# One-hot masks for four tokens in one VectorE operation, the gate weights put on by ScalarE

## The chip, the cores and the metric

One core of one Trainium2 chip. The metric is the device time of one execution, in microseconds (us), the median of the runs. The engines are called PE (TensorE), DVE (VectorE), ACT (ScalarE), POOL (GpSimd) and SP (SyncE, here only a DMA queue).

## What is computed

Two transformer blocks on 256 tokens of width 1024, in float32: a mixer with sparse attention and a state space model, feed-forward layers, a short convolution, a second mixer, and at the end `peer_ffn`, a feed-forward layer over 16384 experts of which each token and head picks 16. The change lies in that last layer:

```python
idx = jnp.take_along_axis(cand_i, pos, axis=-1)      # expert = i1 * 128 + i2
gate = jax.nn.softmax(top_s, axis=-1)
...
hid = jnp.einsum('thkd,td->thk', u[ib], xb)
a = jax.nn.gelu(hid.astype(jnp.float32), approximate=False) * gb
return jnp.einsum('thk,thkd->td', a.astype(x.dtype), v[ib])
```

## The kernel before, in words

The expert layer is computed densely for 224 of the 256 tokens (T): all 16384 experts, 128 at a time, with a matrix of gates that is zero where a token did not pick an expert. The gate matrix of one token is 128 x 128 (first key by second key), and is the product of two matrices with one row for each of its 128 picks: the first row is a one-hot of the first key times the gate, the second a one-hot of the second key. The other 32 tokens are done by fetching the rows of their picks ("picks" below).

The stage that the change touches (`peer_build` in the stream's phases) runs over 56 groups of four tokens. Groups are numbered 0 to 55. In a group:

- DVE, `one_hots(n)`: waits until the scatter of group n - 2 is done (the two buffers alternate), and writes the first one-hots of four tokens into `OH1` (L2780, one operation for a token: compare with `iota`, a row 0 to 127 that lies in PSUM, then multiply by the gate) and the second ones into `OH2` (L2783, one operation for the four). Both are parts of `XN`; `OH1` is `XN[:, 0]`, `OH2` is `XN[:, 1]`. `selT` holds, for each token as a column, the first key, the second key and the gate.
- PE, `scatter`: waits for the one-hots, and multiplies them, four matmuls into one PSUM bank (L1395).
- ACT: copies the first 48 columns of each token's gates out of the bank (L1975).
- DVE, `weigh(n)`: waits for that copy, and multiplies the other 80 into the activations that lie there (L2793).

Six groups of seven also carry one unit of weights (48 units in all, a unit is 128 experts by 1024): a group whose number is divisible by 7 carries none. For each unit a DMA brings 128x1024 floats into a ring of four, ACT rounds each half to the high part (L1475, `round_unit`, called through `follow`, which works two units ahead), POOL subtracts to get the low part (L665), and PE multiplies (L789, L790). ACT then copies the low product out of the bank (L1989, event `build_low`), DVE adds it to the high one (L2805, `summed_build`, event `build_sum`), and ACT takes the gelu of the unit before (L1967, `staged`), which is spilled to memory.

On 20 of the groups DVE also does one pick (L2763): a multiply with a sum over 128x1024, both operands in SBUF. POOL starts the fetch of its rows (L677).

Everything is ordered by hand: each engine runs its own list, and waits on semaphores. DVE's list in this stage is, for n from 2 on, `one_hots(n)`, `weigh(n - 2)`, `summed_build(n - 2)`, and the pick if there is one. `one_hots(0)` and `one_hots(1)` come eight units earlier. ACT's list for group n is the copy L1975, the two roundings of the unit two ahead, the copy L1989, and the gelu L1967. After the stage come 128 units of the last product (L1419, L1421), and the end.

Of the kernel before, what the change touches and what calls it, by code (L numbers as in the profile page):

```python
# [20 lines left out]
ALU = mybir.AluOpType  # L21
ACT = mybir.ActivationFunctionType
# [5 lines left out]
P = 128  # L28
# [39 lines left out]
GROUPS_OF_4 = T // 4  # L68
# [179 lines left out]
def build(nc, stream, x, vec, row, row2, kv_w, br_w, key_w, u_rows, v_rows, gain_row, spill, out):  # L248
    ctx = ExitStack()

    def sb(name, shape, dt=F32):
        return ctx.enter_context(nc.sbuf_tensor(name, shape, dt))

    def sem(name):
        return ctx.enter_context(nc.semaphore(name))

    with ctx:
# [3 lines left out]
        XN = sb("XN", [P, NT, D])  # L261
# [18 lines left out]
        selT = sb("selT", [P, 3, S])  # L280
# [125 lines left out]
        OH1 = XN[:, 0, :].rearrange("p (b n k) -> p b n k", b=2, n=4)  # L406
        OH2 = XN[:, 1, :].rearrange("p (b n k) -> p b n k", b=2, n=4)
# [21 lines left out]
        def ev(name):  # L429
            if name not in events:  # L430
                events[name] = sem(name)
            return events[name]
# [28 lines left out]
        def unit_used(phase, e, i=0):  # L461

            return halves_used, number(phase, e, i, 2, 2)
# [4 lines left out]
        def before_turn(name, i=0):  # L468

            bank, n, _ = TURNS[name]  # L470
            return bank_free[bank], i + n

        def fills(name):
            return bank_full[TURNS[name][0]], 1

        def full(name, i=0):
            bank, _, n = TURNS[name]
            return bank_full[bank], i + (n + 1)
# [4 lines left out]
        def read_out(name, i=0):  # L483

            bank, n, _ = TURNS[name]
            return bank_free[bank], i + (n + 1)

        def bank(name):
            return psum[TURNS[name][0]]
# [238 lines left out]
        def _(pe):  # L728
# [623 lines left out]
            def experts():  # L1352
# [35 lines left out]
                def scatter(g, i):  # L1388

                    j = i * BUILD_GROUPS + g  # L1390
                    name = f"G{j % 4}"
                    pe.wait_ge(*before_turn(name, j // 4))
                    pe.wait_ge(ev("one_hot"), j + 1)
                    for n in range(4):
                        last = mm(bank(name)[:, n * P:(n + 1) * P], OH1[:, j % 2, n, :], OH2[:, j % 2, n, :],  # L1395
                                  start=True, stop=True)
                    last.then_inc(*fills(name))

                for i in range(BUILD_ITERS):
                    for g in range(BUILD_GROUPS):  # L1400
                        scatter(g, i)
                        if g % PERIOD:
                            e = (PERIOD - 1) * (g // PERIOD) + g % PERIOD - 1
# [29 lines left out]
                for half in range(2):  # L1433
                    cols = slice(half * HALF, (half + 1) * HALF)
                    first, second = f"picked_rows{half}", f"picked_rows{2 + half}"
# [3 lines left out]
                    for c in range(4):  # L1439
                        k, at = 4 * half + c, slice(c * P, (c + 1) * P)  # L1440
# [23 lines left out]
        def _(act):  # L1464
            A = nc.scalar.activation
            chain = Chain(act, scalar_chain)

            def round_unit(phase, e, i=0, halves=range(2)):

                act.wait_ge(*unit_in(phase, e, i))  # L1470
                for k in halves:
                    if not isinstance(i, int) or 2 * (PHASES[phase].first + e) + k >= HSLOTS:

                        act.wait_ge(halves_used, number(phase, e, i, 2, k + 1 - HSLOTS))
                    A(w_hi[:, half_slot(phase, e, k), :], ring[:, slot(phase, e), k * HALF:(k + 1) * HALF],  # L1475
                      ACT.Copy).then_inc(rounded, 1)

            def follow(phase, e, i=0, halves=range(2)):

                at = PHASES[phase].first + e + AHEAD + (i * PHASES[phase].units if isinstance(i, int) else 0)  # L1480
                if at < NUNITS:
                    round_unit(phase, e + AHEAD, i, halves)
# [411 lines left out]
            def experts():  # L1894
# [45 lines left out]
                for u in range(EARLY):  # L1940
# [10 lines left out]
                    for t, after in enumerate((32, 58)):  # L1951
                        if u == after:
                            act.wait_ge(ev("top_diff"), t + 1)
                            A(TS[:, t, :, :], TS[:, t, :, :], ACT.Exp,
                              scale=stat[:, 6 + t:7 + t]).then_inc(ev("top_exp"), 1)
# [8 lines left out]
                def staged(c):  # L1964

                    act.wait_ge(ev("build_sum"), c + 1)
                    A(stage[:, c % STAGED, :], bank(f"build{c % 3}")[:, 0:T],  # L1967
                      ACT.Gelu).then_inc(*frees(f"build{c % 3}"))

                act.wait_ge(ev("pick_index_in"), 16 * LANES)  # L1970
                act.wait_ge(ev("pick_gate_in"), 16 * LANES)
                for n in range(GROUPS_OF_4):
                    i, g = n // BUILD_GROUPS, n % BUILD_GROUPS
                    act.wait_ge(*full(f"G{n % 4}", n // 4))
                    A(G[:, 0:GATED, 4 * n:4 * n + 4],  # L1975
                      bank(f"G{n % 4}")[:].rearrange("p (t k) -> p k t", t=4)[:, 0:GATED, :],
                      ACT.Copy).then_inc(ev("gates_copied"), 1)
                    if g % PERIOD:
                        e = (PERIOD - 1) * (g // PERIOD) + g % PERIOD - 1
                        c = i * BUILD_UNITS + e  # L1980
                        follow("peer_build", e, i)
                        if c == GATED - 1:
                            for q in range(4):
                                act.wait_ge(*read_out(f"G{q}", GROUPS_OF_4 // 4 - 1))
                            A(A_hi[:, 0, 0:T], G[:, GATED, :], ACT.Copy).then_inc(ev("late_high"), 1)
                        if c >= STAGED:
                            act.wait_ge(ev(f"spilled{c % STAGED}"), 16 * (c // STAGED))
                        act.wait_ge(*unit_used("peer_build", e, i))
                        A(stage[:, c % STAGED, :], bank(f"build{c % 3}")[:, T:2 * T], ACT.Copy).then_inc(ev("build_low"), 1)  # L1989
                        if c:  # L1990
                            staged(c - 1)
                staged(GATED - 1)
# [49 lines left out]
            mixer2()  # L2042
            norm_late(6, "norm2")
            experts()


        @block.vector
        def _(dve):
            V = nc.vector
# [610 lines left out]
            def experts():  # L2660
# [13 lines left out]
                for t in range(NT):  # L2674
# [40 lines left out]
                    places = psum[3][:, 0:256].rearrange("p (k f) -> p k f", k=2)  # L2715
# [29 lines left out]
                iota = bank("iota")[:, 0:P]  # L2745
# [28 lines left out]
                def one_hots(n):  # L2774

                    if n >= 2:
                        dve.wait_ge(*full(f"G{(n - 2) % 4}", (n - 2) // 4))
                    for k in range(4):
                        tok = 4 * n + k
                        V.tensor_scalar(OH1[:, n % 2, k, :], iota, selT[:, 0, tok:tok + 1],  # L2780
                                        selT[:, 2, tok:tok + 1], ALU.is_equal, ALU.mult)
                    second = selT[:, 1, 4 * n:4 * n + 4]
                    V.tensor_tensor(OH2[:, n % 2, :, :], iota.unsqueeze(1).broadcast_to([P, 4, P]),  # L2783
                                    second.unsqueeze(2).broadcast_to([P, 4, P]),
                                    ALU.is_equal).then_inc(ev("one_hot"), 1)

                def weigh(n):
# [18 lines left out]

                one_hots(0)
                one_hots(1)
                summed_early(8)
                for n in range(2, GROUPS_OF_4):  # L2810
# [186 lines left out]
```

## Time and profile before

| | us |
|---|---|
| median of 3 runs (lowest, highest) | 1683.74 (1679.53, 1688.74) |
| the profiled execution | 1680.42 |
| its span | 1678.7 |
| PE busy | 1630.7 (97%) |
| DVE busy | 1050.8 (63%) |
| ACT busy | 973.3 (58%) |
| POOL busy | 1129.6 (67%) |

The profile counts an engine as busy from the start of an instruction to its end, the last part of which can lie over the next instruction. So a row "x4" of four like instructions is shorter than four times one. Times in the rows are from the start of the span. An idle time in brackets is that just before the instruction, with the instruction that ended it.

### The profile page before, as it was taken

The numbers are of one execution on the slowest core, as the hardware profiler recorded it, in microseconds if no ns is written. First come the engines' busy times: TensorE is split into PE (matmuls) and PEld (weight loads), VectorE is DVE, ScalarE is ACT, GpSimd is POOL, SyncE is SP. The second block draws the span as 40 slices with busy tenths as digits, with TensorE's granted clock in tenths as the row PEclk, the third lists the DMA queues.
The fourth block names the chain that finished last, engine by engine and source line by source line (L and its number), as shares of the span: only waits on it lengthen the run. The fifth ranks groups of instructions, "written<-read, shape, count | busy, mean of one in ns | idle before, by whom it ended". The sixth has DMA issues, their size and how long they took to land.

```text
span 1678.7 us, 30573 instructions
## 1 busy us (share of the span) xinstructions
PE 1630.7 (97%) x10334; PEld 1489.0 (89%) x10334; DVE 1050.8 (63%) x2318; ACT 973.3 (58%) x1962; POOL 1129.6 (67%) x897
## 2 busy tenths in 40 slices
PE   8999999999999999999999999998999999999998
PEld 8888888889988888899998989998899899998997
DVE  2784433334243333754523589995999888787997
ACT  5556655555465555666545667665555566665664
POOL 8445799998989999886536799998888711111110
PEclk9999999999999999999999999999999999999999
DMA  6333455554545555443333465655677788788994
GB/s 231 102 107 108 156 188 189 188 187 169 187 165 190 187 187 190 168 155 138 127 151 118 161 215 194 205 200 203 209 249 236 234 276 301 268 278 285 325 333 162
DMA packets 102012, 332.52 MB, mean 198 GB/s; under 512 B 11888, under 2 KB 24304, under 8 KB 101648
## 3 DMA queue, kind: packets, MB, share of 16 engines
q1 hardware_dynamic: 91152, 292.07, 50.5%
q0 software_dynamic: 9696, 37.91, 7.4%
q10 hardware_dynamic: 1056, 1.16, 0.3%
q8 instruction: 60, 0.98, 0.2%
q14 instruction: 48, 0.39, 0.1%
HBM read 323.98 MB, written 6.55 MB: 197 GB/s over the span
## 4 chain that ended last, share of the span: by engine, by line
PE 72%; POOL 9%; DVE 9%; issue 6%; ACT 2%; DMA 1%; POOLq 0%; SPq 0%; DVEq 0%; ACTq 0%
PE bank L757 27%; PE bank L789 12%; PE bank L1419 12%; POOL w_lo L665 9%; PE bank L790 6%; PE bank L1421 6%; DVE XN L2780 3%; DVE arena L2763 1%; PE bank L735 1%; DVE XN L2783 1%; DMA ring<-stream 1%; PE bank L1395 1%; PE bank L1307 1%; DVE arena L2793 1%; ACT w_hi L1475 1%
## 5 line engine op out<-in xcount | busy, mean ns | idle before, releaser
L665 POOL TENSOR_TENSOR w_lo<-ring,w_hi 128x512 fp32r<-128x512 f32 x804 | 1045.7, 1318 | 249.5 <-ACT w_hi L1475 214.1
L1475 ACT ACTIVATE w_hi<-ring 128x512 fp32r<-128x512 f32 x1060 | 662.8, 630 | 524.9 <-PE bank L790 239.9
L789 PE MATMUL bank<-h_high_and_low,w_hi 128*128 128x448 f32 (+1 forms) x1728 | 584.2, 389 | 8.8 <-POOL w_lo L665 8.8
L790 PE MATMUL bank<-h_high_and_low,w_lo 128*128 128x224 f32 (+1 forms) x1728 | 468.4, 271 | 0.0
L789 PEld LDWEIGHTS bank<-h_high_and_low,w_hi 128*128 128x128 f32 x1728 | 326.0, 189 | 59.7 <-POOL w_lo L665 12.4
L790 PEld LDWEIGHTS bank<-h_high_and_low,w_lo 128*128 128x128 f32 x1728 | 329.7, 191 | 1.6
L1419 PE MATMUL bank<-A_high_and_low,w_hi 128*128 128x448 f32 x1024 | 322.9, 376 | 4.4 <-DVE A_high_and_low L2835 4.3
L757 PE MATMUL bank<-h_high_and_low,w_hi 128*128 128x256 f32 x1504 | 286.3, 288 | 4.2 <-POOL w_lo L665 3.5
L1421 PE MATMUL bank<-A_high_and_low,w_lo 128*128 128x224 f32 x1024 | 270.0, 264 | 0.0
L757 PEld LDWEIGHTS bank<-h_high_and_low,w_hi 128*128 128x128 f32 x1504 | 241.2, 194 | 7.7 <-issue 3.8
L757 PE MATMUL bank<-h_high_and_low,w_lo 128*128 128x256 f32 x752 | 214.8, 286 | 0.0
L1419 PEld LDWEIGHTS bank<-A_high_and_low,w_hi 128*128 128x128 f32 x1024 | 192.7, 188 | 20.2 <-DVE A_high_and_low L2835 5.2
L1421 PEld LDWEIGHTS bank<-A_high_and_low,w_lo 128*128 128x128 f32 x1024 | 195.9, 191 | 0.0
L2828 DVE TENSOR_TENSOR w_lo<-ring,w_hi 128x512 fp32r<-128x512 f32 x256 | 175.9, 689 | 30.2 <-ACT w_hi L1475 19.7
L677 POOL DMA_INDIRECT arena<-v_rows,rows x32 | 37.5, 1172 | 191.4 <-DVE arena L2770 158.2
L757 PEld LDWEIGHTS bank<-h_high_and_low,w_lo 128*128 128x128 f32 x752 | 146.3, 195 | 1.0 <-issue 0.7
L757 PE MATMUL bank<-w_hi,A_high_and_low 128*128 128x512 f32 x432 | 143.0, 392 | 0.6 <-DVE A_high_and_low L2460 0.3
L2452 DVE TENSOR_TENSOR bank<-bank,arena 128x256 f32<-128x256 f32 x44 | 19.0, 433 | 146.5 <-ACT arena L1751 146.3
L757 PE MATMUL bank<-w_hi,h_high_and_low 128*128 128x512 f32 (+1 forms) x336 | 102.5, 379 | 2.3 <-POOL w_lo L665 2.0
L757 PEld LDWEIGHTS bank<-w_hi,A_high_and_low 128*128 128x128 f32 x432 | 81.1, 188 | 19.7 <-DVE A_high_and_low L2460 1.2
L2009 ACT ACTIVATE A_high_and_low<-arena 128x224 fp32r<-128x224 f32 x127 | 49.6, 391 | 63.8 <-PE bank L1421 60.7
L757 PE MATMUL bank<-w_lo,A_high_and_low 128*128 128x512 f32 x216 | 84.6, 392 | 0.0
(387 smaller groups left out, 1906.6 us busy)
## 6 DMA issues: line engine op xcount, KB each, us to landing
ring<-stream SPq DMA_DIRECT2D x530, 512.0 KB
spill<-mask_parts SPq DMA_DIRECT2D x48, 112.0 KB
XN<-spill SPq DMA_DIRECT2D x48, 112.0 KB, 5.7
arena<-branch_w POOLq DMA_DIRECT2D x1, 3072.0 KB, 12.9
X<-x SPq DMA_DIRECT2D x2, 512.0 KB, 4.8
arena<-kv_w SPq DMA_DIRECT2D x1, 1024.0 KB, 6.7
out<-X SPq DMA_DIRECT2D x4, 256.0 KB, 2.2
arena<-row POOLq DMA_DIRECT2D x1, 512.0 KB, 4.5
```

The source lines that it names most:

```text
L665: nc.gpsimd.tensor_tensor(w_lo[:, hs, :], ring[:, slot(phase, e), k * HALF:(k + 1) * HALF], w_hi[:, hs, :].bitcast(F32), ALU.subtract) \
L677: nc.gpsimd.indirect_dma_start(fetched[:, s % FETCH, :], None, (u_rows if s < PICKED else v_rows), bass.IndirectOffsetOnAxis(pick_index[:, ...
L757: last = mm(dst, a, b, start=start and n == 0, stop=stop and n == 2, skip_group_check=True)
L789: mm(dst[:, 0:2 * n], high, h[:, k, :, 0:n], start=k == 0, stop=False, skip_group_check=True)
L790: last = mm(dst[:, 0:n], low, h_hi[:, k, 0:n], start=False, stop=k == KC - 1, skip_group_check=True)
L1419: mm(dst[:, 0:2 * T], high, A2[:, :, n % 2, 0:T], start=n == 0, stop=False, skip_group_check=True)
L1421: last = mm(dst[:, 0:T], low, A_hi[:, n % 2, 0:T], start=False, stop=n == NKEYS - 1, skip_group_check=True)
L1475: A(w_hi[:, half_slot(phase, e, k), :], ring[:, slot(phase, e), k * HALF:(k + 1) * HALF], ACT.Copy).then_inc(rounded, 1)
L2009: A(A_hi[:, nxt % 2, 0:T], chunk(GATED + nxt if nxt < EARLY else nxt - EARLY), ACT.Copy).then_inc(ev("late_high"), 1)
L2452: chain(V.tensor_tensor(gate[:, 0:S], gate[:, 0:S], LOW[:, q % 2, 0, :], ALU.add))
L2780: V.tensor_scalar(OH1[:, n % 2, k, :], iota, selT[:, 0, tok:tok + 1], selT[:, 2, tok:tok + 1], ALU.is_equal, ALU.mult)
L2828: V.tensor_tensor(w_lo[:, hs, :], ring[:, slot(phase, e), k * HALF:(k + 1) * HALF], w_hi[:, hs, :].bitcast(F32), ALU.subtract) \
```

## The change

DVE compares `iota` with the first and the second keys of four tokens in one operation over 128x1024 elements, which gives both masks as zeros and ones. ACT multiplies the first mask by the gates in place, one operation for a token (`weighted`), and counts `first_weighted`. PE's scatter waits for that instead of `one_hot`. ACT does groups 0 and 1 ahead of its loop, and group n + 2 right after the copy of group n. The rounding of a unit's second half moves behind the copy L1989 (L2002 in the changed kernel).

```diff
@@ scatter
-                    pe.wait_ge(ev("one_hot"), j + 1)
+                    pe.wait_ge(ev("first_weighted"), j + 1)
@@ ACT
+                def weighted(n):
+
+                    if n < GROUPS_OF_4:
+                        act.wait_ge(ev("one_hot"), n + 1)
+                        for k in range(4):
+                            tok = 4 * n + k
+                            ins = A(OH1[:, n % 2, k, :], OH1[:, n % 2, k, :], ACT.Copy,
+                                    scale=selT[:, 2, tok:tok + 1])
+                        ins.then_inc(ev("first_weighted"), 1)
+
+                weighted(0)
+                weighted(1)
                 for n in range(GROUPS_OF_4):
...
                       ACT.Copy).then_inc(ev("gates_copied"), 1)
+                    weighted(n + 2)
                     if g % PERIOD:
...
-                        follow("peer_build", e, i)
+                        follow("peer_build", e, i, (0,))
...
                         A(stage[:, c % STAGED, :], bank(f"build{c % 3}")[:, T:2 * T], ACT.Copy).then_inc(ev("build_low"), 1)
+                        follow("peer_build", e, i, (1,))
                         if c:
                             staged(c - 1)
@@ DVE, one_hots
-                    for k in range(4):
-                        tok = 4 * n + k
-                        V.tensor_scalar(OH1[:, n % 2, k, :], iota, selT[:, 0, tok:tok + 1],
-                                        selT[:, 2, tok:tok + 1], ALU.is_equal, ALU.mult)
-                    second = selT[:, 1, 4 * n:4 * n + 4]
-                    V.tensor_tensor(OH2[:, n % 2, :, :], iota.unsqueeze(1).broadcast_to([P, 4, P]),
-                                    second.unsqueeze(2).broadcast_to([P, 4, P]),
+                    both = XN[:, :, n % 2 * 4 * P:(n % 2 + 1) * 4 * P].rearrange("p w (n k) -> p w n k", n=4)
+                    places = selT[:, 0:2, 4 * n:4 * n + 4]
+                    V.tensor_tensor(both, iota.unsqueeze(1).unsqueeze(1).broadcast_to([P, 2, 4, P]),
+                                    places.unsqueeze(3).broadcast_to([P, 2, 4, P]),
                                     ALU.is_equal).then_inc(ev("one_hot"), 1)
```

ACT's list at the begin of the stage, before. The first row is the last of the stage ahead; L1975 is the copy of a group's gates (groups 0 and 1, then 2), L1475 the two roundings, L1989 the copy of the low product, L1967 the gelu:

```order
L1919 ACTIVATE arena<-bank 128x224 x2
L1975 ACTIVATE arena<-bank 128x48x4 x2
L1475 ACTIVATE w_hi<-ring 128x512 x2
L1989 ACTIVATE mask_parts<-bank 128x224
L1975 ACTIVATE arena<-bank 128x48x4
L1475 ACTIVATE w_hi<-ring 128x512 x2
L1989 ACTIVATE mask_parts<-bank 128x224
L1967 ACTIVATE mask_parts<-bank 128x224
```

The same place now; L1978 puts the gates on (groups 0 and 1 at the head, then 2, 3, 4), L1987 is the copy of the gates, L2002 the copy of the low product:

```order
L1919 ACTIVATE arena<-bank 128x224 x2
L1978 ACTIVATE XN<-XN,selT 128x128 x8
L1987 ACTIVATE arena<-bank 128x48x4
L1978 ACTIVATE XN<-XN,selT 128x128 x4
L1987 ACTIVATE arena<-bank 128x48x4
L1978 ACTIVATE XN<-XN,selT 128x128 x4
L1475 ACTIVATE w_hi<-ring 128x512
L2002 ACTIVATE mask_parts<-bank 128x224
L1475 ACTIVATE w_hi<-ring 128x512
L1987 ACTIVATE arena<-bank 128x48x4
L1978 ACTIVATE XN<-XN,selT 128x128 x4
L1475 ACTIVATE w_hi<-ring 128x512
```

Four operations of ACT now stand between the copy of a group's gates and the copy of a unit's low product, and the second rounding stands behind that.

DVE's list from group 1's sum on, before (then all of one pass, with its pick, and the next masks; L2780 and L2783 the one-hots, L2793 `weigh`, L2805 `summed_build`, L2763 the pick):

```order
L2805 TENSOR_TENSOR bank<-bank,mask_parts 128x224
L2780 TENSOR_SCALAR XN<-bank,selT 128x128 x4
L2783 TENSOR_TENSOR XN<-bank,selT 128x512
L2793 TENSOR_TENSOR arena<-arena,bank 128x80x4
L2805 TENSOR_TENSOR bank<-bank,mask_parts 128x224
L2763 SCALAR_TENSOR_TENSOR arena,rows<-arena 128x1024
L2780 TENSOR_SCALAR XN<-bank,selT 128x128 x4
L2783 TENSOR_TENSOR XN<-bank,selT 128x512
```

And now (L2794 both masks, L2804 `weigh`, L2816 `summed_build`, L2777 the pick):

```order
L2816 TENSOR_TENSOR bank<-bank,mask_parts 128x224
L2794 TENSOR_TENSOR XN<-bank,selT 128x2x512
L2804 TENSOR_TENSOR arena<-arena,bank 128x80x4
L2816 TENSOR_TENSOR bank<-bank,mask_parts 128x224
L2777 SCALAR_TENSOR_TENSOR arena,rows<-arena 128x1024
L2794 TENSOR_TENSOR XN<-bank,selT 128x2x512
```

Five operations have become one, and the order of the rest stands: the sum of a unit, and the pick, still come ahead of the next group's masks.

## Rows read from the trace of the kernel before

**Rows 1.** Busy time by stretch: stretch, length, busy PE, PEld, DVE, ACT, POOL, clock, DMA
```profile
1180.00:1200.00 20.00, 19.08 (x138) 18.31 (x137) 20.00 (x52) 11.15 (x30) 17.72 (x14) 1.00 0.65 214
...
1380.00:1500.00 120.00, 119.86 (x765) 114.07 (x764) 98.76 (x168) 73.33 (x145) 19.46 (x17) 1.00 0.82 281
```

**Rows 2.** Groups by shape, 1160 to 1338 us: busy us, mean ns, idle before
```profile
L1395 PE MATMUL bank<-XN 128*128 128x128 f32 x444 | 59.3, 277 | 8.3 <-DVE XN L2783 8.2
L2763 DVE SCALAR_TENSOR_TENSOR arena<-arena 128x1024 f32<-128x1024 f32 x20 | 36.8, 1839 | 0.0
```

**Rows 3.** Timeline of DVE, one group with a unit: start us, length us
```profile
1221.09 1.36 DVE L2780 TENSOR_SCALAR XN<-bank,selT 128x128 f32<-128x128 f32 x4
1222.38 0.68 DVE L2783 TENSOR_TENSOR XN<-bank,selT 128x512 f32<-128x512 f32 x1
1222.97 0.47 DVE L2793 TENSOR_TENSOR arena<-arena,bank 128x320 f32<-128x320 f32 x1
1223.37 0.39 DVE L2805 TENSOR_TENSOR bank<-bank,mask_parts 128x224 f32<-128x224 f32 x1
1223.67 1.35 DVE L2780 TENSOR_SCALAR XN<-bank,selT 128x128 f32<-128x128 f32 x4
```

**Rows 4.** The chain of waits in order of time: start us, length us
```profile
1233.78 0.90 PE bank L1395 x8
1237.18 0.90 PE bank L1395 x8
```

**Rows 5.** Timeline of ACT: the first gate copies, and part of a group
```profile
1161.21 0.55 ACT L1975 ACTIVATE arena<-bank 128x192 f32<-128x192 f32 x2
...
1202.06 0.63 ACT L1475 ACTIVATE w_hi<-ring 128x512 fp32r<-128x512 f32 x1 [0.56 <-PE bank L790]
1202.60 0.34 ACT L1989 ACTIVATE mask_parts<-bank 128x224 f32<-128x224 f32 x1
1202.83 0.35 ACT L1967 ACTIVATE mask_parts<-bank 128x224 f32<-128x224 f32 x1
```

**Rows 6.** Timeline of ACT, much earlier: two 128x128 operations with a scale per partition
```profile
917.54 0.68 ACT L1492 ACTIVATE XN<-ident,stat 128x128 f32<-128x128 f32 x2
918.13 1.92 ACT L1475 ACTIVATE w_hi<-ring 128x512 fp32r<-128x512 f32 x3
```

**Rows 7.** Timelines of ACT and DVE: hand-overs between the two
```profile
1167.78 0.34 ACT L1989 ACTIVATE mask_parts<-bank 128x224 f32<-128x224 f32 x1
1168.22 0.40 DVE L2805 TENSOR_TENSOR bank<-bank,mask_parts 128x224 f32<-128x224 f32 x1 [0.19 <-ACT mask_parts L1989]
1176.10 0.39 DVE L2805 TENSOR_TENSOR bank<-bank,mask_parts 128x224 f32<-128x224 f32 x1
1176.52 0.36 ACT L1967 ACTIVATE mask_parts<-bank 128x224 f32<-128x224 f32 x1 [1.61 <-DVE bank L2805]
```

**Rows 8.** Timeline of ACT: the low copy of the stage's last unit
```profile
1341.15 0.34 ACT L1989 ACTIVATE mask_parts<-bank 128x224 f32<-128x224 f32 x1
```

**Rows 9.** Timelines of POOL and DVE around the first pick and the eighth
```profile
1165.30 7.52 POOL L665 TENSOR_TENSOR w_lo<-ring,w_hi 128x512 fp32r<-128x512 f32 x6
1168.53 5.38 DVE L2763 SCALAR_TENSOR_TENSOR arena<-arena 128x1024 f32<-128x1024 f32 x1
1225.74 1.28 POOL L665 TENSOR_TENSOR w_lo<-ring,w_hi 128x512 fp32r<-128x512 f32 x1
1226.24 1.87 DVE L2763 SCALAR_TENSOR_TENSOR arena<-arena 128x1024 f32<-128x1024 f32 x1
```

**Rows 10.** Timeline of PE at two stalls, and stretches around the first (columns as rows 1)
```profile
1147.62 0.47 PE L789 MATMUL bank<-h_high_and_low,w_hi 128*128 128x448 f32 x1 [2.41 <-POOL w_lo L665]
1141.00:1160.00 19.00, 15.91 (x92) 14.62 (x91) 6.61 (x18) 9.77 (x23) 16.10 (x13) 0.91 0.49 167
1149.00:1150.00 1.00, 1.00 (x6) 0.91 (x5) 0.02 (x1) 0.11 (x1) 1.00 (x2) 0.50 0.30 45
1175.93 1.13 PE L1395 MATMUL bank<-XN 128*128 128x128 f32 x8 [1.93 <-DVE XN L2783]
```

## The prediction, made before the changed kernel ran

> **What bounds the kernel now.** First the busy time by stretch, to see which engine fills the stage. From 1180 to 1200 us, inside the stage, DVE is busy 20.00 of 20.00 us and PE 19.08, at full clock [rows 1]. After the stage PE is busy 119.86 of 120 us [rows 1]: whatever the stage gains or loses stays in the total, since PE has nothing to catch up with. Then the groups: PE's scatter waited 8.2 us for one-hots [rows 2]. The timeline gives what each step costs in DVE's row of work, start to start: first one-hots 1.29, second 0.59, `weigh` 0.40, sum 0.30; together 2.58 us for a group with a unit, 2.28 without [rows 3]. The 20 picks add 36.8 us [rows 2]: 48 x 2.58 + 8 x 2.28 + 36.8 = 179 us, which is the stage. PE by itself needs 3.40 us for a group with a unit, since two scatters start 1233.78 and 1237.18, 0.90 of it the scatter [rows 4]: 48 x 3.40 + 8 x 0.90 = 170.4 us. So DVE bounds the stage, about 10 us above PE.
>
> **What the change takes away and adds.** DVE: five operations of 1.29 + 0.59 = 1.88 us become one of 128x1024. That shape is not there with one operand in PSUM. The 128x512 one takes 0.68 and the 128x320 one 0.47 [rows 3], so 512 elements more are 0.54, and one takes 1.21 us (start to start 1.12). Bounds: a 128x1024 row with both operands in SBUF has a mean of 1.84 [rows 2], two of 128x512 are 1.35. I take 1.21, for the new operation has the operands of L2783. DVE's row falls by 0.76 us a group, 43 us in all, far below PE. Alone that would be a gain.
>
> ACT: four operations of 128x128 with a scale per partition. Two such started 0.59 us before what followed them [rows 6]: 0.295 each, start to start, and 0.68 for both means 0.39 for the last. From below, a 128x224 copy without such a scale takes 0.23 start to start [rows 5]; from above, four of 0.39 with no overlap. I take 0.295, the same form of instruction. So four cost 1.18 us.
>
> **Who waits for that.** ACT's row stays under PE's: 0.2 for the gates, 1.18, two roundings of 0.54, copy and gelu 0.24 each [rows 5], 2.9 us. But the order of waits closes a loop through DVE and ACT in every group with a unit. ACT can't copy the low product of group m before it has put the gates on group m + 2; for that it needs DVE's masks m + 2; these stand in DVE's list behind the sum of group m - 1 and its pick; and that sum waits for the low copy of group m - 1. One turn of the loop per group, with nothing to run ahead. Its length:
> - low copy 0.34 [rows 7];
> - hand-over to DVE 0.10 (1167.78 + 0.34 to 1168.22) [rows 7];
> - sum 0.30, start to start [rows 3];
> - both masks 1.21;
> - hand-over to ACT 0.04 (1176.10 + 0.39 to 1176.52), with the other direction's 0.10 as its upper bound [rows 7];
> - four with the gates 1.18;
> - first rounding 0.54, to the next low copy [rows 5].
>
> Together 3.71 us, against PE's 3.40. Before, there was no such loop: ACT's low copy did not wait for one-hots. A pick now lies on the loop with its full length, where it was only one more piece of DVE's row. By itself a pick takes about as long as now: it starts 0.74 us after the low copy (0.34 + 0.10 + 0.30); POOL is then in the half whose rounding ended 0.09 after that copy's start, until about 1.47 (1.28 us [rows 9]); and a pick ends 1.09 after such a POOL operation (1225.74 + 1.28 to 1226.24 + 1.87) [rows 9], at 2.56. That is 1.82, start to start 1.75. A group without a unit adds masks and `weigh`, 1.12 + 0.40 = 1.52.
>
> **The sum.** The gates of group 0 can only go on once ACT has finished the stage ahead, at 1161.21, where the first gate copy now starts [rows 5]; before, PE scattered by itself. From there: 1.27 (3 x 0.295 + 0.39) and 0.1, scatter 0.90, then 0.1; masks of group 2 and `weigh` 1.52; masks of group 3 1.21; gates 1.18; rounding 0.54: the first low copy starts 6.9 later, at 1168.1. Then 45 turns of 3.71 = 167.0; the last two low copies have no gates ahead of them and go by PE, 2 x 3.40 = 6.8; 20 picks x 1.75 = 35.0; 7 groups without a unit x 1.52 = 10.6. The last low copy starts at 1387.5. Now it starts at 1341.15 [rows 8]. So +46 us on the profiled execution: 1680.4 + 46.4 = **1727 us**, 2.7% slower. The median of the runs shown is 3.3 us above the profiled execution; the sum is made against the latter.
>
> Moved at no cost: the second rounding goes 0.24 us back, behind the low copy, and waits for the same thing, the end of the group's unit. POOL has it 0.9 us after the low copy's start, and PE has to begin on that half by about 6 us after it (7.4 - 1.25, below); without that cover the loop would wait for PE. SP's loads follow POOL's splits, which only get further apart.
>
> **The clock.** PE's granted clock fell to 0.50 of full, the 1.2 GHz level, after a stall of 2.41 us, and did not fall at the stall of 1.93 that ends at 1175.93 [rows 10]. In the changed kernel PE waits about 0.3 us a group, and where a pick and a group without a unit come together 2 to 4 us, perhaps ten times, so it will fall there. One fall costs PE some 1.7 us of work (19 us at a mean of 0.91) [rows 10]. I price that at nothing: PE is off the loop, with about 3 us to spare. (Two halves split by POOL at 1.28, the second then multiplied in 1.25, end some 4.1 us after the low copy of group m; the low copy of group m + 2 wants them at 7.4.) The Trainium skill speaks of more (TensorE: Matmul & The Clock Gate, "A second HAM failure mode: psum-queue depth-cycling"): PE that idles briefly between groups of matmuls makes the clock swing between its levels, and throughput drops. By that rule PE itself could get slower than the loop; that is the third rival, and of it the one fall in [rows 10] is all that the trace shows.
>
> **The picks and POOL.** The first pick ran into a block of six POOL operations on end and took 5.38 us, to 1.1 after the block's end at 1172.82; the eighth waited for one operation only [rows 9]. In the changed kernel the second rounding is ready 0.5 us before POOL's first half ends, so POOL again has work on end. If DVE loses that hand-over each time, a pick takes 1.2 us more. The Trainium skill (SBUF — State Buffer, "Who interferes with whom") has DVE and GpSimd take a shared pair of ports for one whole instruction, the other blocked till its end; by that alone a pick waits for one POOL operation, 1.75 us as above, and the sum stands. The first pick disagrees with it, the eighth agrees.
>
> **The rivals.**
> - The gates cost ACT less. If the four go at the pace of plain copies, 0.23 as the 128x224 one or 0.14 by number of elements, the loop is 3.45 to 3.1 us and the total 1715 down to 1699. For it: plain copies of ACT do go at that pace [rows 5]. Against: the same form as the new one does not [rows 6]. Chance 0.12 for below 1715.
> - The loop doesn't hold, and PE bounds the stage: 170.4 + 3 us later start against 181 now (1161 to 1341.15 is 180), some 8 us less, **1672 us**. For it: DVE's row falls to 2.58 - 0.76 = 1.82 a group and ACT's stays under 3.40. The point from which it decides: from the first low copy at 1168.1 to the present last one there are 173.0 us, so a turn must be under (173.0 - 6.8 - 35.0 - 10.6) / 45 = 2.7 us. It would have to be a whole microsecond shorter, nearly all that the four gate operations cost; or ACT would have to have the masks a group ahead, which the order of DVE's list forbids. Chance 0.05. About the same as before, within 0.5%: 0.04.
> - PE's clock swings and PE becomes the bound. Ten to fifteen falls that no longer hide cost 1.7 each, 17 to 25 us more: 1744 to 1752. Against it: PE's 3 us to spare. Chance 0.07.
> - DVE loses the hand-over to POOL at the picks: 20 x 1.2 = 24 us, 1751. Chance 0.06.
>
> **How the numbers follow.** The forecast's own case has 0.66. Its bounds: hand-over to ACT up by 0.06 is +3; masks of 1.35 instead of 1.21 +6, of 1.84 +28; a mean pick of 1.2 or 2.1 instead of 1.75 -11 or +7; gates with no overlap +17. The range of 1703 to 1750 takes these in but for the dearest masks, which have two SBUF operands, half of the first rival and most of the third, and leaves out the fast case, no change, and the far ends, under 0.2. A measurement of this kernel tells about 0.5% (8 us) from no change, as the runs shown lie within 0.3% of their median: faster 0.05, same 0.04, slower 0.91.
>
> **What would show it.** In the changed profile: the low copies (L2002) 3.7 us apart in groups with a unit and no pick, 5.4 with one, and the last at about 1387; the masks (L2794) at 1.21 us; L1978 at 0.39 with four in 1.27; each L1978 released by DVE's L2794, each DVE sum by ACT; DVE busy some 60% of the stage (56 x 1.52 + 48 x 0.30 + 35 = 134 of 226 us) and PE near 75% (170 of 226); the chain of waits going back and forth between ACT and DVE. Wrong would be: PE without stalls at the scatter, 3.40 us between scatters, or L1978 starting without an idle time ahead of it.

## The result, and the profile after

The changed kernel takes 1720.61 us (median of 4 runs, 1720.04 to 1722.21), against 1682.21 us for the kernel before in the same series (1679.53 to 1688.74). The ratio is 1.0224, 95% interval 1.0194 to 1.0253: slower by 38.4 us. The profiled execution took 1722.21 us (span 1720.4), that of before 1680.42, so between the two traces that are compared here there are 41.8 us; the forecast was +46.4, and 1727. Among the runs of the versions below there is one of 1974.29 us, at a granted clock of 0.752, which stands in no median and no ratio here.

The page after, its busy time, the chain that ended last (shares of the span by line), and the group of the new operation (busy us, mean ns, idle before it):

```profile
PE 1649.1 (96%) x10334; PEld 1500.2 (87%) x10334; DVE 1011.0 (59%) x2094; ACT 1032.2 (60%) x2186; POOL 1137.9 (66%) x897
...
PE bank L757 26%; PE bank L1419 12%; PE bank L789 12%; POOL w_lo L665 9%; PE bank L790 6%; PE bank L1421 6%; DVE XN L2794 3%; ACT XN L1978 2%; ACT w_hi L1475 2%; PE bank L735 1%; PE bank L1395 1%; DVE bank L2816 1%; PE bank L1307 1%; DVE arena L2777 1%; PE bank L836 1%
...
L1978 ACT ACTIVATE XN<-XN,selT 128x128 f32<-128x128 f32 x224 | 71.6, 391 | 65.6 <-DVE XN L2794 65.5
```

DVE's masks, ACT's gates and ACT's first rounding now stand one behind the other on the chain. In order of time (start us, length us):

```profile
1175.51 0.40 DVE bank L2816
1175.91 1.14 DVE XN L2794
...
1177.38 0.97 ACT XN L1978 x3
1178.35 0.52 ACT w_hi L1475
1178.88 0.25 ACT mask_parts L2002
```

Busy time by stretch (columns as [rows 1]), inside the stage and behind it:

```profile
1160.00:1380.00 220.00, 191.06 (x1203) 178.48 (x1203) 135.17 (x197) 153.26 (x461) 154.02 (x118) 0.92 0.57 187
1380.00:1500.00 120.00, 119.30 (x760) 113.28 (x759) 98.53 (x175) 73.51 (x146) 18.61 (x19) 1.00 0.84 282
```

Against [rows 1]: DVE, which was busy without a gap, is now busy 61% of the stage, no engine is full in it, and the stage is 41 us longer. Behind it PE is as full as before, so the loss stays in the total. The last low copy starts at 1382.02, against 1341.15 [rows 8]: 40.9 of the 41.8 us lie ahead of it.

The groups of the stage by shape, 1160 to 1380 us (busy us, mean ns, idle before), which answer to [rows 2]:

```profile
L1978 ACT ACTIVATE XN<-XN,selT 128x128 f32<-128x128 f32 x218 | 69.8, 391 | 65.6 <-DVE XN L2794 65.5
L1395 PE MATMUL bank<-XN 128*128 128x128 f32 x446 | 66.2, 297 | 22.4 <-ACT XN L1978 22.4
L2794 DVE TENSOR_TENSOR XN<-bank,selT 128x1024 f32<-128x1024 f32 x54 | 65.6, 1215 | 3.6 <-PE bank L1395 3.6
L2777 DVE SCALAR_TENSOR_TENSOR arena<-arena 128x1024 f32<-128x1024 f32 x20 | 34.7, 1737 | 0.0
L2816 DVE TENSOR_TENSOR bank<-bank,mask_parts 128x224 f32<-128x224 f32 x47 | 18.8, 400 | 82.1 <-ACT mask_parts L2002 78.6 <-PE bank L790 3.6
```

Two waits that face each other are how a loop looks in such a table: DVE's sum waits 78.6 us for ACT's low copy, ACT's gates wait 65.5 us for DVE's masks. One turn of it in the timelines, ACT first, then DVE (start us, length us, idle before):

```profile
1175.07 0.34 ACT L2002 ACTIVATE mask_parts<-bank 128x224 f32<-128x224 f32 x1
1175.31 0.62 ACT L1475 ACTIVATE w_hi<-ring 128x512 fp32r<-128x512 f32 x1
1175.83 0.34 ACT L1967 ACTIVATE mask_parts<-bank 128x224 f32<-128x224 f32 x1
1176.07 0.32 ACT L1987 ACTIVATE arena<-bank 128x192 f32<-128x192 f32 x1
1177.07 1.28 ACT L1978 ACTIVATE XN<-XN,selT 128x128 f32<-128x128 f32 x4 [0.68 <-DVE XN L2794]
1178.26 0.62 ACT L1475 ACTIVATE w_hi<-ring 128x512 fp32r<-128x512 f32 x1
1178.78 0.34 ACT L2002 ACTIVATE mask_parts<-bank 128x224 f32<-128x224 f32 x1
```

```profile
1170.07 0.40 DVE L2816 TENSOR_TENSOR bank<-bank,mask_parts 128x224 f32<-128x224 f32 x1 [1.78 <-ACT mask_parts L2002]
1170.38 1.81 DVE L2777 SCALAR_TENSOR_TENSOR arena<-arena 128x1024 f32<-128x1024 f32 x1
1172.12 0.08 DVE L2777 DVE_READ_ACCUMULATOR arena<-arena 128x1 f32 x1
1172.12 1.21 DVE L2794 TENSOR_TENSOR XN<-bank,selT 128x1024 f32<-128x1024 f32 x1
1173.26 0.47 DVE L2804 TENSOR_TENSOR arena<-arena,bank 128x320 f32<-128x320 f32 x1
1175.51 0.40 DVE L2816 TENSOR_TENSOR bank<-bank,mask_parts 128x224 f32<-128x224 f32 x1 [1.79 <-ACT mask_parts L2002]
1175.82 1.22 DVE L2794 TENSOR_TENSOR XN<-bank,selT 128x1024 f32<-128x1024 f32 x1
```

Low copy 1175.07, sum 1175.51, masks 1175.82, gates 1177.07, rounding 1178.26, next low copy 1178.78: 3.71 us. The turn before it has the pick of 1170.38 in it and takes 5.43. Over the stage, 24 turns take 3.70, 14 with a pick 5.42 to 5.44, and 7 across a group without a unit 5.2 to 7.0.

### The profile page after: what moved, and what is told of

It is laid out like the page before. It is cut to its first block, busy times and chain, and to the rows that moved or that the text cites. A ratio compares the mean times of both kernels' runs of the same rounds, so it can differ in the third digit from the quotient of the medians.

```text
span 1720.4 us, 30621 instructions
## 1 busy us (share of the span) xinstructions
PE 1649.1 (96%) x10334; PEld 1500.2 (87%) x10334; DVE 1011.0 (59%) x2094; ACT 1032.2 (60%) x2186; POOL 1137.9 (66%) x897
## 4 chain that ended last, share of the span: by engine, by line
PE 70%; POOL 9%; DVE 7%; issue 6%; ACT 6%; DMA 1%; POOLq 0%; DVEq 0%; ACTq 0%; SPq 0%
PE bank L757 26%; PE bank L1419 12%; PE bank L789 12%; POOL w_lo L665 9%; PE bank L790 6%; PE bank L1421 6%; DVE XN L2794 3%; ACT XN L1978 2%; ACT w_hi L1475 2%; PE bank L735 1%; PE bank L1395 1%; DVE bank L2816 1%; PE bank L1307 1%; DVE arena L2777 1%; PE bank L836 1%
## 5 line engine op out<-in xcount | busy, mean ns | idle before, releaser
L1475 ACT ACTIVATE w_hi<-ring 128x512 fp32r<-128x512 f32 x1060 | 661.4, 629 | 456.8 <-PE bank L757 218.6
L789 PE MATMUL bank<-h_high_and_low,w_hi 128*128 128x448 f32 (+1 forms) x1728 | 592.9, 393 | 14.8 <-POOL w_lo L665 14.4
L677 POOL DMA_INDIRECT arena<-v_rows,rows x32 | 42.9, 1341 | 186.3 <-DVE arena L2784 153.5
L1978 ACT ACTIVATE XN<-XN,selT 128x128 f32<-128x128 f32 x224 | 71.6, 391 | 65.6 <-DVE XN L2794 65.5
L1395 PE MATMUL bank<-XN 128*128 128x128 f32 x448 | 66.5, 297 | 25.5 <-ACT XN L1978 25.5
```

Source lines behind the costliest of these rows:

```text
L677: nc.gpsimd.indirect_dma_start(fetched[:, s % FETCH, :], None, (u_rows if s < PICKED else v_rows), bass.IndirectOffsetOnAxis(pick_index[:, ...
L789: mm(dst[:, 0:2 * n], high, h[:, k, :, 0:n], start=k == 0, stop=False, skip_group_check=True)
L1978: ins = A(OH1[:, n % 2, k, :], OH1[:, n % 2, k, :], ACT.Copy, scale=selT[:, 2, tok:tok + 1])
```

## The experiments

Each is an edit of the changed kernel and runs against the kernel before; "turn" is the distance from one low copy to the next. The ratio and its 95% interval are against the kernel before in the same series, whose median was 1682.12 to 1685.01 us. That the time went into the loop is the theory. The rivals are PE's clock, the amount of ACT's added work by itself, and the picks.

**Gates late.** `weighted(n + 2)` goes to the end of ACT's pass, behind the low copy and the second rounding. The work is the same; the loop is opened.

```
-                    weighted(n + 2)
                     if g % PERIOD:
...
                             staged(c - 1)
+                    weighted(n + 2)
```

> The gates of group m + 2 go on at the end of ACT's pass for group m instead of ahead of the first rounding and the low copy; nothing is left out. Loop theory: the low copy of group m no longer waits for DVE's masks m + 2, one turn of the loop now spans two groups (3.7 us plus a gate copy, against 6.8 of PE), so PE bounds the stage: 48 x 3.40 + 8 x 0.90 = 170.4 us from the first scatter, about 51 us less than in the changed kernel, 1670 to 1676 us, and so 6 to 12 us below the kernel before. Rival A (ACT has simply too much to do, the four operations delay the roundings): the same work in another order gives the same time, 1720. Rival B (PE's clock falls are the loss): about 17 us of the 41 come back, near 1704, unless the stalls go too.

1688.28 us (1684.71 to 1692.7), ratio 1.0029 (1.0009 to 1.0049). Of the 40 turns that don't cross a group without a unit 36 are 3.40 us, with or without a pick (the other four 3.23 to 3.93), and the low copies now wait for PE:

```profile
1164.90 0.36 ACT L2001 ACTIVATE mask_parts<-bank 128x224 f32<-128x224 f32 x1 [0.40 <-PE bank L790]
1168.30 0.36 ACT L2001 ACTIVATE mask_parts<-bank 128x224 f32<-128x224 f32 x1 [0.56 <-PE bank L790]
```

So 32 of the 38 us come back by order alone, at the same 224 gate operations. It fell short of the expectation by 12 us or more, at one place: across a group without a unit the turn is 6.15 to 6.7 instead of 4.30, 14 us in all. PE gets through the empty group in 0.9 us and then waits for gates that ACT has only reached after the unit ahead (PE's timeline, the three scatters around such a group):

```profile
1201.45 1.06 PE L1395 MATMUL bank<-XN 128*128 128x128 f32 x8
1204.85 1.06 PE L1395 MATMUL bank<-XN 128*128 128x128 f32 x8
1207.54 1.13 PE L1395 MATMUL bank<-XN 128*128 128x128 f32 x8 [1.62 <-ACT XN L1978]
```

**Pick ahead.** DVE's pick goes ahead of its sum, the gates stay early.

```
                     weigh(n - 2)
-                    summed_build(n - 2)
                     if n in PICK_GROUPS:
                         pick(PICK_GROUPS.index(n))
+                    summed_build(n - 2)
```

> In DVE's list the pick stands ahead of the sum instead of behind it, where DVE now waits 1.78 us for the low copy; nothing is left out. Loop theory: 16 of the 20 picks fall into that wait and leave the loop, 16 x 1.73 = 28 us less, 1693 us; the four in groups without a unit stay. Sums of a group with a pick start 3.7 us after the last, no longer 5.4. Rival A (ACT's load): no change, 1720. Rival B (clock): the longest stalls of PE come with the picks, so most of the falls go, and with them up to 17 us, 1704.

1694.46 us (1690.41 to 1698.75), ratio 1.0061 (1.0036 to 1.0086). Nearly all turns with a pick fell from 5.43 to 3.70, the others stayed. DVE's row of work shows why: the pick now fills the time in which DVE waits for the low copy anyway, and only 0.35 us of that wait is left:

```profile
1233.19 1.51 DVE L2777 SCALAR_TENSOR_TENSOR arena<-arena 128x1024 f32<-128x1024 f32 x1
1234.62 0.08 DVE L2777 DVE_READ_ACCUMULATOR arena<-arena 128x1 f32 x1
1235.06 0.40 DVE L2816 TENSOR_TENSOR bank<-bank,mask_parts 128x224 f32<-128x224 f32 x1 [0.35 <-ACT mask_parts L2002]
```

The same 20 operations are worth 26 us by standing one instruction further on or back; from the first low copy to the last it is 188.3 us instead of 216.1.

**Two gates.** Only two of the four gate operations are left in each group; the gates of the other two tokens are left out.

```
-                        for k in range(4):
+                        for k in range(2):
```

> ACT puts the gates on the first two tokens of a group only; the other two keep plain masks, so their gates are left out. All else as in the changed kernel. Loop theory: a turn is two operations of 0.295 shorter, 3.11 us, and 4.84 with a pick; 45 turns and the first groups give 27 us less, 1694 us. Where DVE's wait for the low copy shrinks (1.78 to 1.19 us) nothing else changes. Rival A (ACT's load: half of the 66 us of added work goes, spread over what ACT delays): some part of the 38 us, not a fixed 0.59 a turn. Rival C (PE waits for the gates themselves, not the loop): the start to start of low copies goes to PE's 3.40.

1703.19 us (1700.63 to 1705.63), ratio 1.0114 (1.0084 to 1.0144); 9 us over what was expected. A plain turn took 3.11 us, 0.59 less, as two operations at 0.295 ask; a turn with a pick 4.84. But three picks took 3.5 us instead of 1.8 (5.3 us in all, see the last section), and three of the seven crossings of a group without a unit shrank by 0.04 to 0.19 only. The loop's length is confirmed; my count of how often it alone decides was too high.

**Both halves first.** Both roundings stand ahead of the low copy again, as before the change.

```
-                        follow("peer_build", e, i, (0,))
+                        follow("peer_build", e, i)
...
-                        follow("peer_build", e, i, (1,))
```

> Both roundings stand ahead of the low copy, as in the kernel before; all else as in the changed kernel. Loop theory: the second rounding joins the loop with 0.54 us (0.52 in the changed kernel's rows), 45 turns, 23 to 24 us more, 1744 us. Rival A (ACT's load): the same work, 1720. Rival C (PE waits for the second halves, which the change made late): earlier second halves make it faster than 1720.

1735.52 us (1733.1 to 1740.2), ratio 1.0314 (1.0284 to 1.0344). Low copies in ACT's timeline:

```profile
1232.81 0.34 ACT L2002 ACTIVATE mask_parts<-bank 128x224 f32<-128x224 f32 x1
1237.03 0.34 ACT L2002 ACTIVATE mask_parts<-bank 128x224 f32<-128x224 f32 x1
1241.26 0.33 ACT L2002 ACTIVATE mask_parts<-bank 128x224 f32<-128x224 f32 x1
1246.66 0.33 ACT L2002 ACTIVATE mask_parts<-bank 128x224 f32<-128x224 f32 x1
```

A plain turn is 4.22, exactly one rounding (0.52) longer. A turn with a pick stayed at 5.42: the pick now starts 1.09 us into POOL's split instead of 0.57, and takes 1.26 instead of 1.80 (it is POOL's next split that is stretched, to 2.26). So from the first low copy to the last the kernel took 13.0 us more, 229.1 for 216.1, and not 23 to 24; the median missed by 8. By the medians the split of the two roundings in the change is worth 15 us, and without it the change would have cost 53.

**More work for PE.** Two of the four products of a scatter are made twice.

```
-                    for n in range(4):
+                    for n in (0, 1, 0, 1, 2, 3):
```

> PE does two of a group's four scatter matmuls twice, 0.45 us more work per group, 25 us in all; the result is the same. Loop theory: PE is off the loop with about 3 us to spare, so no change, 1720 to 1723; with 3.85 us a group PE needs 48 x 3.85 + 8 x 1.35 = 196 us, still under the stage's 221. Rival B (PE or its clock bounds the stage): 25 us more, 1745, or less than that if the added work keeps the clock up.

1723.8 us (1721.41 to 1725.17), ratio 1.0245 (1.0215 to 1.0275): 3 us more for 25 us of added PE work, 0.8 above the expected range. From the first low copy to the last it is 216.7 us against 216.1. The turns are 3.70 and 5.43 as before, and in the stage PE is busy 201.76 us:

```profile
1160.00:1380.00 220.00, 201.76 (x1399) 193.35 (x1400) 133.98 (x193) 151.22 (x456) 151.73 (x114) 0.95 0.58 184
```

PE has time to spare, so neither its work nor its clock sets the stage. The clock, at 0.92 of full in the changed kernel, even rose to 0.95 as PE's gaps were filled.

**No gates.** ACT puts no gates on (they are left out), and PE's scatter waits for the masks.

```
                 def weighted(n):
-                    if n < GROUPS_OF_4:
...
+                    return
...
-                    pe.wait_ge(ev("first_weighted"), j + 1)
+                    pe.wait_ge(ev("one_hot"), j + 1)
```

> ACT puts no gates on at all, and PE's scatter waits for DVE's masks; the gates of the dense part are left out. This is DVE's side of the change alone, with the second rounding where the change put it. Loop theory: without the link through ACT there is no loop; the stage is PE's, from a first scatter near 1156.5 (3 us earlier than now, for it no longer waits for ACT) 170.4 us, 1668 to 1674 us. The slow start of e1 and its stalls at the groups without a unit (1.6 us, 8 times) are gone with the gates. If the moved rounding or the wider mask operation cost something by themselves, this stays above 1682.

1675.68 us (1672.04 to 1677.66), ratio 0.9946 (0.9925 to 0.9968). Nearly all turns are 3.40, and 4.29 across a group without a unit: PE alone sets these. It stands slightly above the range, for the first pick took 7.67 us and made one turn of 8.75. Without that, a placing of the gates could at best come some 5 us below this time, an estimate from 8.75 less 3.40.

**Late but one.** As gates late, but early where the next group has no unit, and gates 0 and 1 inside the stage ahead.

```
                     follow(phase, at % 4, at // 4)
+                    if u in (EARLY - 5, EARLY - 3):
+                        weighted((u - EARLY + 5) // 2)
...
-                    weighted(n + 2)
+                    early = (n + 1) % PERIOD == 0
+                    if early:
+                        weighted(n + 2)
                     if g % PERIOD:
...
+                    if not early:
+                        weighted(n + 2)
```

> As e1 (gates of group m + 2 at the end of ACT's pass for group m), but where group m + 1 has no unit they go on at once, as in the changed kernel, and the gates of groups 0 and 1 go on during the stage ahead. Nothing is left out. e1 lost 1.6 us of PE at each of the 8 groups without a unit, since PE passes these in 0.90 us and ACT's gates for the next came 2.3 us after the unit, and 3.1 us at the first scatter. Loop theory: the loop closes once in seven groups only, 0.3 us, or 2.0 with a pick, which PE's spare time takes; so both losses go: 1684.1 - 13 - 3 in the profile, 1668 to 1674 us, faster than both kernels. Rival A (ACT's load, 2.9 of 3.40 us in a group with a unit): it stays near 1685, with PE waiting for gates elsewhere.

1682.71 us (1680.31 to 1686.42), ratio 0.9998 (0.9982 to 1.0013): missed by 9 us or more. Most turns are 3.24 to 3.40. But the first pick is long (turns of 7.47 and 4.84). And where the loop is closed, once in seven groups, the turn is 4.07 to 4.09 without a pick, 0.7 above PE's and not the 0.3 that I had counted, and with one 5.1 to 6.5, or 5.6 in the crossing behind it. POOL's and DVE's rows of work at the first pick:

```profile
1166.47 7.50 POOL L665 TENSOR_TENSOR w_lo<-ring,w_hi 128x512 fp32r<-128x512 f32 x6
```

```profile
1168.52 6.53 DVE L2781 SCALAR_TENSOR_TENSOR arena<-arena 128x1024 f32<-128x1024 f32 x1 [0.47 <-DMA arena<-u_rows,rows]
```

**The same with the pick ahead**, as in pick ahead.

> As e8, with DVE's pick ahead of the sum as in e2. Loop theory: where the loop is broken the picks no longer lie on any path that matters, so the same as e8 within 3 us. If picks still delay ACT's masks where the loop closes (once in seven groups), this is up to 5 us less than e8.

1679.95 us (1677.06 to 1683.81), ratio 0.9971 (0.9954 to 0.9987), 2.8 us less than late but one. That fits both cases of the expectation (the same within 3 us, or up to 5 less), so it doesn't tell them apart; in the traces it is 178.3 us from the first low copy to the last, against 182.2. Its first pick took 6.92 us.

**Late but one, picks two groups later.**

```
-PICK_GROUPS = [4 + 5 * s // 2 for s in range(20)]
+PICK_GROUPS = [6 + 5 * s // 2 for s in range(20)]
```

> The kernel of e8_late_but_one with every pick two groups later (first in the list of group 6 instead of 4). In e8 the first pick took 6.53 us: it met six operations of POOL on end (7.50 us), with which POOL made up what it had left while it issued the first three fetches; the low copies around it are 7.47 us apart. If that backlog is what stretches it, the pick two groups later takes 1.2 to 1.8 us, the turn is under 5 us, and the kernel takes 3 to 5 us less than e8: 1678 to 1680. If the first pick is long for a reason of its own (its first use of the fetched rows), it stays at 6 to 7 us wherever it stands, and the time stays at 1682 to 1683.

1680.29 us (1677.01 to 1683.34), ratio 0.9975 (0.9956 to 0.9995). The fetches behind the first three move with the picks, as they are counted from the same list. The first pick is short, though it too fell into a block of POOL:

```profile
1176.21 1.23 DVE L2781 SCALAR_TENSOR_TENSOR arena<-arena 128x1024 f32<-128x1024 f32 x1
```

```profile
1167.52 11.08 POOL L665 TENSOR_TENSOR w_lo<-ring,w_hi 128x512 fp32r<-128x512 f32 x8
```

Its turn took 3.40. So its length does not come from its being the first, nor from POOL's block alone: here it started 1.13 us into one of the block's splits, in late but one 0.81 (see the last section). Against late but one the median is 2.4 us lower, the ratio 0.0023 (4 us), and from the first low copy to the last it is 177.6 us against 182.2. That is about what was expected, though the two intervals of the ratio overlap.

**Gates between the halves.** As gates late, with gates 0 and 1 in the stage ahead, the pick ahead and two groups later, and this for the group that was late:

```
                         A(stage[:, c % STAGED, :], bank(f"build{c % 3}")[:, T:2 * T], ACT.Copy).then_inc(ev("build_low"), 1)
+                        if early:
+                            weighted(n + 2)
                         follow("peer_build", e, i, (1,))
```

> The kernel of e1_gates_late with three things changed: gates 0 and 1 are put on inside the stage ahead, the gates of the group after one without a unit stand between the low copy and the second rounding (so the low copy never waits for masks, and these gates are 0.54 us earlier), and each pick stands ahead of the sum and two groups later. No loop of waits goes through a low copy then. If the loop and the first pick's backlog are all that kept the time up, low copies are 3.40 us apart and 4.30 to 5.4 across a group without a unit, the last at 1330 to 1338: 1669 to 1677, 0.4 to 0.9% under the kernel before. If POOL is the next bound (its split of the second half comes 1.2 us later), PE waits at L789 and the time stays at 1680 to 1684, as e9.

1679.74 us (nine runs of 1675.79 to 1683.96), ratio 0.9967 (0.9949 to 0.9986): 3 us above the range. Nearly all turns are 3.40, but 5.39 across a group without a unit, and one is 8.53, with a pick of 4.08 in it. PE does not wait for POOL there (the rival), but 0.9 to 1.0 us for gates, 2.39 at the long one, and a low copy waits for PE.

Three versions of the order thus end 0.25 to 0.33% under the kernel before, and 2.4% under the change as it was made. By their intervals the first is a real difference, but a small one, and no trace shows where it lies: from the first low copy to the last they took 178.3, 177.6 and 177.9 us, the kernel before 176.8 in its one trace, which is among its fastest executions (1680.42, against medians of 1682 to 1685). Only no gates, with 173.4, is below it there. With DVE relieved, PE's 170 us are the stage's floor, and before the change the stage took 180 (1161 to 1341).

## Why the prediction was right

**Direction and cause.** The loop is there, place by place: its turn is 3.70 us against 3.71, with a pick 5.43 against 5.46 (3.71 + 1.75). Opening it on ACT's side (gates late) or taking the picks off it brought back 32 and 26 us; making PE dearer brought no change in its turns. The parts that could not be seen before came out at the values taken: the masks 1.215 us for 1.21, the gates 0.391 for 0.39 with four in 1.28 for 1.27. The Trainium skill (ScalarE: Activation LUTs, "What ACT_TABLE_LOAD costs") gives 186 ns + 0.833 ns an element, 93 for an operand by pointer, and 93 of overlap. For 128 elements an estimate from these figures is 386 ns and a step of 293, and the trace agrees with 391 and 295.

**Picks.** Sixteen took 1.78 to 1.81, priced at 1.82 (start to start 1.73, priced at 1.75). The four in passes without a sum took 1.49 to 1.51, for which there was no separate price. None lost a hand-over to POOL, so that rival fell.

**The size, 5.5 us too high at the last low copy** (1382.02 for 1387.5). Three terms, of which the first is a gain that was not foreseen and the second a loss that was priced at nothing; that they partly cancel is luck:
- The start, 2.2 too late (1165.94 for 1168.1). The term took ACT free at 1161.21, where it was before. It was free at 1158.00, 3.2 us earlier. Of these, 0.6 stood already when DVE began on the first masks (1140.57 against 1141.18), which is no effect of the change that the runs show: in the traces of the experiments this point lies at 1141.2 to 1144.6. For the rest I had counted the change's gain on DVE inside the stage and not for groups 0 and 1, whose one-hots stand in the stage ahead. There DVE took 3.75 us for them (1141.18 to 1144.93) and now 2.27; the stall of 2.41 [rows 10] is one of 1.42, and the fall of the clock that followed it is gone. Eight of the ten experiments have this stall at 1.40 to 1.42 too. In the other two (both halves first, picks two groups later) it is 2.28 and 2.27 with the same masks ahead of it; so the change alone does not fix its length, and what does stays open. DVE's and PE's timelines of the changed kernel, and then its stretch (columns as [rows 1]), whose clock was 0.91 before and is 0.99:

```profile
1140.57 2.34 DVE L2794 TENSOR_TENSOR XN<-bank,selT 128x1024 f32<-128x1024 f32 x2
...
1146.02 0.47 PE L789 MATMUL bank<-h_high_and_low,w_hi 128*128 128x448 f32 x1 [1.42 <-POOL w_lo L665]
```

```profile
1141.00:1160.00 19.00, 13.79 (x86) 12.57 (x85) 4.92 (x10) 12.70 (x33) 17.15 (x15) 0.99 0.56 191
```

- Against that, from ACT's first gates to the first low copy it took 7.94 instead of 6.9. PE had waited 3.11 us for the gates, and its clock fell to 0.50, the 1.2 GHz level, during the first two scatters; the first gate copy of G had to wait for that. "I price that at nothing" failed for this one fall: it was on the path. (By the text, falls were hidden since PE is off the loop; at the start there is no loop yet.) Gates late shows what it cost: after the same stall of 3.11 the clock stayed at 1.00 there, and the two scatters took 2.30 us instead of 3.52. PE's and ACT's timelines, and one of the stretches:

```profile
1159.41 3.52 PE L1395 MATMUL bank<-XN 128*128 128x128 f32 x16 [3.11 <-ACT XN L1978]
...
1161.27 0.33 ACT L1987 ACTIVATE arena<-bank 128x192 f32<-128x192 f32 x1 [0.83 <-PE bank L1395]
```

```profile
1160.00:1161.00 1.00, 1.00 (x6) 1.00 (x6) 0.00 (x0) 0.44 (x2) 0.84 (x1) 0.50 0.24 45
```

- The 45 turns with picks and empty groups took 210.6 instead of 212.6, and the last two 5.5 instead of 6.8, since PE was ahead by some work when the loop let go. (The prediction's terms from 1161.21 to the first low copy add up to 6.8, not 6.9.)

**The clock inside the stage** was off in its share, not in its price. PE was to be busy near 75% and was busy 87%: it did what the prediction counted as 170 us of work at full clock in 191, at a mean clock of 0.92. Those 20 us fell into time in which PE would have waited for gates. More work for PE showed this directly: 25 us of added matmuls changed no turn. By the Trainium skill's rule on brief idling (TensorE: Matmul & The Clock Gate, "A second HAM failure mode: psum-queue depth-cycling") PE's throughput drops in such a case, and it did; it cost nothing as PE was not the bound.

**The gain on DVE** was real, 0.76 us a group, and nothing of it arrived. DVE's idle time rose to 85 us in the stage.

## What to carry to other kernels

Before moving work from a full engine to one with room, follow the new hand-over around: if the receiver's wait stands ahead of something for which the giver waits, in their fixed orders, there is a loop, and its turn is the sum of all it passes, however idle both engines are. Two large waits that name each other are its mark in a profile, and moving one instruction past another, with no work saved, can be worth more than a cheaper instruction: here 32 and 26 us. Price what the change does ahead of the stage as well, and where the next engine's floor lies: here 10 us under the present time, so that even the best order could win only about that.

## What the runs showed of the hardware that was not expected

**How long a pick takes depends on when in POOL's operation it starts.** In all twelve traces of this study, for picks that start x us into a POOL split: if POOL has no further split on end behind it, the pick takes 2.37 - x, but not under 1.22 (2.09 at 0.28, 1.87 at 0.51, 1.50 at 0.86). If POOL has more on end, a start at 0.51 to 0.58 gives 1.78 to 1.87, and POOL's next operation is the one that is stretched (a split from 1.28 to 2.3 us). A start at 0.66 to 0.82 was lost in 21 of 22 cases, and then to all of POOL's operations up to the gap: 2.8 us with one more behind, 4.1 with two, 5.38 with three [rows 9], 6.53 with four. A start at 0.05 to 0.18 lost one operation and then won (3.5). Elsewhere both were seen: 2.07 at 0.31 and 6.92 at 0.43, 1.44 at 0.92 and 7.67 at 0.91. The picks of the changed kernel are even because the loop always starts them 0.57 or 0.86 into POOL's operation.

The Trainium skill (SBUF — State Buffer, "SBUF: two separate sides") has the shared pair go to whichever starts first for one instruction. The picks without more work on end agree with it; those of 4 to 8 us, which let two to five POOL operations pass, do not. What decides who gets the next turn stays open: no run here changed the start alone. It also says that a DVE operation is concerned if both its inputs are in SBUF. The masks have one in PSUM, and all 54 in the stage of the changed kernel took 1.21 to 1.23 us whatever POOL did, against 1.21 to 7.67 for the picks of the same shape in the twelve traces.

**Gates late, late but one, and no gates all speed the stage up to where these long picks return**: in each some take 2.8 us or more, in the changed kernel none. Making the stage faster thus brought back a cost that the slow loop had hidden.
